# A two-layer streaming encoder on one core: the loop over MLP groups in pairs, squares on ScalarE with a tree of additions, xlo moved by 64 bytes, GpSimd's lower halves in four pieces, and later stores of x

## The chip, the cores and the metric

The kernel runs on one core of a Trainium2 chip. The metric is the device time of one execution in microseconds, and lower is better. The engines are TensorE (PE in the profile; PEld is its loading of weights), VectorE (DVE), ScalarE (ACT), GpSimd (POOL) and SyncE (SP), which here only issues transfers. They run side by side, each with its own instruction stream, and meet at semaphores.

## The reference, cut to what matters

```python
def rms_norm(x, g):
    return x * rsqrt(mean(x * x, axis=-1) + 1e-6) * g

# for each of DEPTH = 2 layers; x is 256 prompt rows and 64 sample rows of 2048
h = rms_norm(x, g_mix)
A | B | C | D = split(h @ w_in)              # four groups of attention heads, four kinds of attention
x = x + concat(oa, ob, oc, od) @ w_out
x = x + square(relu(rms_norm(x, g_mlp) @ w_up)) @ w_down        # 2048 -> 8192 -> 2048
x = x + (ple @ w_ple) * sigmoid(rms_norm(x, g_ple) @ w_ple_gate)
```

All is float32. The three norms need, for each of the 320 rows, the sum of 2048 squares; the division by the root comes after the product with the weights, so the matmuls can start on x times the gain.

## The kernel before, in words

**Layout.** x is feature-major: 16 blocks (KB) of 128 features on the partitions, each with 320 columns (TOK: 256 prompt and 64 sample rows), so 5120 floats or 20480 bytes in each partition. A float32 product is made of three matmuls in fp32r on a high and a low half of both operands (`product`, L695 to L697): low weight half by high x half, high by low, high by high. The upper half of the weights is made by ScalarE (`whi`, a Copy that rounds, L1130), the lower by GpSimd (`wlo = ring - whi`, L659). xhi and xlo are made by VectorE (`split_blocks`, L1351 and L1354), hhi and hlo in the MLP's up projection (L1752 and a product, L1313), pleh and plel for the embeddings.

**Where the halves lie.** xlo starts at 4 x KB x TOK = 20480 bytes behind xhi. plel starts 2560 bytes behind pleh. Adding up the allocations between them, hlo starts 145344 bytes behind hhi. xhi, xlo and the buffers of the attention share memory; the end of xlo meets the start of probT.

**Weights.** SyncE loads them as units of 512 KB into `ring`, which has four slots (RING). The layer's list of units (STREAM) starts with the 12 units of group A's columns of w_in (N_UP = 12), then come B, D, C, the latent weights and w_out, 108 units in all (TAIL0); the tail is 300 units: the end of w_out, the MLP, w_ple and w_ple_gate. In the head (up to TAIL0) a slot is loaded again when PE has used its unit, and the lower half is made in place, in pieces of 256 columns (`lower_in_place`, L646). In the tail a slot is loaded again as soon as both halves are made. ScalarE converts up to three units ahead of PE.

**The order on SyncE** is written out by hand in `beside`: ahead of the load of unit 4 stand 25 small loads of vectors and caches, and ahead of the loads of units SAVE_AT to SAVE_AT + 3 (5 to 8) stands one store of four blocks of x to DRAM each (L547). x is needed again when w_out is added (loaded back at BACK_AT), and the first copy of B's columns (`copy_chunk` for chunk 2) overwrites it, so that waits for the stores.

**A layer** runs so. (1) ScalarE makes xw, the rounded x times the gain, VectorE makes xv, its low half (L1324, L1326). Then VectorE takes the first squares: one product over all 5120 columns into the arena, one reduction over the 16 blocks (L1339) and a short copy. PE needs this sum after unit 7. Group A is copied out by VectorE (L1375, L1377), ScalarE squares it for its norm (L1144), and PE waits for that norm before it prepares the heads. ScalarE converts the units up to N_UP + LEAD - 1 = 14 before it takes those squares. (2) Attention in eight jobs, with matmuls for the other groups between. (3) The end of w_out, split and squares for the MLP. (4) The MLP in four groups of 2048 hidden features (FG = 4): a loop on each engine, and in each group four chunks of up (8 units each, `gemm_chunk`) and four of down. A unit is 24 matmuls. PE's loop body for one group is 1536 matmuls, each with its load of weights. VectorE's loop over the groups has a base for its step counter (`here`, UP_STEPS). (5) The embeddings (four units), then the gate in four chunks: meanwhile VectorE splits x again, and after that takes the squares (`squares_pass`: a product over 5120 columns, L1313, and a reduction, L1345). PE needs this sum after the gate's first chunk (`rms_feature`, L739).

Of the kernel before, what the change touches and what calls it, by code (L numbers as in the profile page):

```python
# [16 lines left out]
TOK = SEQ + DSEQ  # L17
# [6 lines left out]
KB = DM // 128  # L24
UK = 2
XW = 256 + 128
RING = 4
FG = FF // DM
# [34 lines left out]
def build(nc, I, O):  # L63
    f32 = mybir.dt.float32
    ALU, ACT, AX = mybir.AluOpType, mybir.ActivationFunctionType, mybir.AxisListType
    X = AX.X
    ctx = ExitStack()
    with ctx:
# [13 lines left out]
        def sem(name):  # L82
            return ctx.enter_context(nc.semaphore(name))
# [26 lines left out]
        xlo = sb("xlo", [128, KB, TOK], f32r, at + 4 * KB * TOK)  # L110
        assert at + 8 * KB * TOK <= top[0]
# [85 lines left out]
        sq_ready = sem("sq_ready")  # L197
        ssq_ready = sem("ssq_ready")
# [137 lines left out]
        SAVE_AT = RING + 1  # L336
# [291 lines left out]
        def _(pool):  # L628
# [9 lines left out]
            with pool.Fori(0, DEPTH) as l:  # L638
# [18 lines left out]
                def lower_half(u4, s):  # L657
                    hold(hi_ready, l * HL + N_WU + RING * u4 + s + 1)
                    nc.gpsimd.tensor_tensor(wlo[:, s, :], ring[:, s, :], whi[:, s, :].bitcast(f32), ALU.subtract)\  # L659
                        .then_inc(lo_ready, 1)  # L660
# [13 lines left out]
        def _(pe):  # L674
# [306 lines left out]
            with pe.Fori(0, DEPTH) as l:  # L981
# [43 lines left out]
                with pe.Fori(0, FG) as g:  # L1025
# [78 lines left out]
        def _(act):  # L1104
# [149 lines left out]
            with act.Fori(0, DEPTH) as l:  # L1254
                act.wait_ge(mix_loaded, 16 * (l + 1))
                gain_pass(l)
                halves(l, range(4, 11))
# [30 lines left out]
                for i in range(9):  # L1288
                    upper_halves(l, Q_PLE + i)
                    if i and i % 2 == 1 and i > 2:  # L1290
                        c = (i - 3) // 2
                        if c == 0:
                            rms_root(l, 1 + FG, ps[:, 7, 0:TOK], rroot[:, :])
                        sigmoids(l, c)
# [4 lines left out]
        def _(dve):  # L1299
# [35 lines left out]

            def first_squares(l):

                done(mul(plout, x[:, :, :], x[:, :, :]))
                done(V.tensor_reduce(acc[:, 0:TOK], plout.rearrange("p b t -> p t b"), X, ALU.add))  # L1339
                V.tensor_copy(acc[:, TOK:], acc[:, 256:TOK]).then_inc(acc_ready, 1)  # L1340

            def squares_pass(l, chunks):
                dve.wait_ge(half_free, l * CHUNKS + 2 + chunks)
                done(mul(hid[:, :, :], x[:, :, :], x[:, :, :]))
                V.tensor_reduce(acc[:, 0:TOK], hid[:, :, :].rearrange("p b t -> p t b"), X, ALU.add).then_inc(acc_ready, 1)  # L1345
# [322 lines left out]
            with dve.Fori(0, DEPTH) as l:  # L1668
# [64 lines left out]
                UP_STEPS = 2 * KB - 4  # L1733
                with dve.Fori(0, FG) as g:
                    here[0] = l * STEPS + g * UP_STEPS
                    at0 = count[0]
# [17 lines left out]
                    assert count[0] - at0 == UP_STEPS  # L1754
                    for c in range(4):
                        add_chunk(l, MLP0 + 32 + 64 * g + 8 * c, 8 + 8 * g + c, c % 2, 4 * c)
                here[0] = l * STEPS
                count[0] += (FG - 1) * UP_STEPS

# [12 lines left out]
                squares_pass(l, 4 + 8 * FG)  # L1772
# [85 lines left out]
```

## Time and profile before

| | |
|---|---|
| Median of 3 runs | 3578.41 us (3575.25 to 3582.28) |
| The profiled execution | 3571.53 us, its span 3569.7 us |
| PE busy | 3371.3 us, 94% of the span |
| DVE, ACT, POOL busy | 1417.0, 1124.7, 1898.2 us |
| Mean granted clock of PE | 0.966 of full speed |
| Chain that ended last, by engine | PE 85%, DVE 7%, issue 4% |

The profile is of one execution. The granted clock has two levels here, 1.2 and 2.4 GHz. The busy time of a matmul overlaps the next one's, so the pace of PE is read from the starts. "Issue" as a releaser means that the engine waited for nothing that the profile shows. Layer 0 is in the span from about 30 to 1789 us, layer 1 from there to 3556.

### The profile page before, as it was taken

The page shows a single profiled execution, that of the slowest core. Times are in us where ns is not written, and L with a number is a line of the kernel's source. Part 1 is how long each engine was busy: PE and PEld are TensorE (multiplying, and loading weights), DVE is VectorE, ACT ScalarE, POOL GpSimd, SP SyncE. Part 2 cuts the span into 40 slices and gives each one's busy share as a digit, 9 for nine tenths or more (in the row PEclk, how much of TensorE's full clock was granted, in tenths as well). Part 3 has the DMA queues.
Part 4 walks back from the last instruction along what each step waited for, and adds up shares of the span by engine and source line. Part 5 has one row for each costly group of instructions (what it writes and reads, how often), then busy time and mean ns, then how long its engine had stood idle before and what let it go on. Part 6 is the DMA issues. An engine that isn't in the chain of part 4 may idle for free.

```text
span 3569.7 us, 58680 instructions
## 1 busy us (share of the span) xinstructions
PE 3371.3 (94%) x20676; PEld 3041.9 (85%) x20676; DVE 1417.0 (40%) x2287; ACT 1124.7 (32%) x1614; POOL 1898.2 (53%) x1189
## 2 busy tenths in 40 slices
PE   7999989999999999999979998989999999999988
PEld 5776756699999999998967776667999999999988
DVE  5334554473052240525362345445621503305163
ACT  2333332333333323332333332313323333333322
POOL 4554200267667676677565551002776676666664
PEclk9999998999999999999989999989999999999999
DMA  5343322244454444544343333223544444445433
GB/s 167 104 118 102 113 66 80 81 137 152 142 148 153 137 153 142 148 154 142 116 136 112 115 95 101 75 71 93 148 154 141 149 154 140 150 144 151 151 122 119
DMA packets 295728, 453.18 MB, mean 127 GB/s; under 512 B 36336, under 2 KB 111344, under 8 KB 294832
## 3 DMA queue, kind: packets, MB, share of 16 engines
q1 hardware_dynamic: 295328, 448.66, 41.2%
q8 instruction: 190, 3.11, 0.3%
q0 software_dynamic: 144, 0.87, 0.1%
q14 instruction: 66, 0.54, 0.0%
HBM read 435.54 MB, written 14.06 MB: 126 GB/s over the span
## 4 chain that ended last, share of the span: by engine, by line
PE 85%; DVE 7%; issue 4%; ACT 1%; DMA 1%; SPq 1%; POOL 0%; DVEq 0%; ACTq 0%; POOLq 0%
PE ps L697 19%; PE ps L696 19%; PE ps L695 19%; PE ps L793 5%; PE ps L781 5%; PE ps L756 4%; PE ps L759 4%; PE ps L758 3%; PE ps L885 1%; DMA ring<-in_w_in 1%; DVE xhi L1351 1%; PE ps L831 1%; PE ps L920 1%; PE ps L889 1%; DVE xlo L1354 1%
## 5 line engine op out<-in xcount | busy, mean ns | idle before, releaser
L659 POOL TENSOR_TENSOR wlo<-ring,whi 128x1024 fp32r<-128x1024 f32 x600 | 1478.1, 2465 | 1256.4 <-ACT whi L1130 1256.4
L1130 ACT ACTIVATE whi<-ring 128x1024 fp32r<-128x1024 f32 x600 | 635.0, 1060 | 1420.9 <-PE ps L697 1420.9
L695 PE MATMUL ps<-xhi,wlo 128*128 128x320 f32 x2560 | 801.6, 313 | 23.4 <-issue 16.4
L696 PE MATMUL ps<-xlo,whi 128*128 128x320 f32 x2560 | 796.5, 311 | 0.0
L697 PE MATMUL ps<-xhi,whi 128*128 128x320 f32 x2560 | 796.4, 311 | 0.0
L697 PE MATMUL ps<-hhi,whi 128*128 128x320 f32 x2176 | 675.5, 310 | 0.0
L695 PE MATMUL ps<-hhi,wlo 128*128 128x320 f32 x2176 | 663.1, 305 | 6.0 <-DVE plel L1727 6.0
L696 PE MATMUL ps<-hlo,whi 128*128 128x320 f32 x2048 | 629.8, 308 | 0.0
L646 POOL TENSOR_TENSOR rlo<-ring,whi 128x256 fp32r<-128x256 f32 (+2 forms) x576 | 416.3, 755 | 371.6 <-ACT whi L1114 371.1
L695 PEld LDWEIGHTS ps<-xhi,wlo 128*128 128x128 f32 x2560 | 485.9, 190 | 28.8 <-issue 27.0
L696 PEld LDWEIGHTS ps<-xlo,whi 128*128 128x128 f32 x2560 | 486.0, 190 | 1.0 <-issue 0.4
L697 PEld LDWEIGHTS ps<-xhi,whi 128*128 128x128 f32 x2560 | 485.4, 190 | 0.0
L756 PE MATMUL ps<-rlo,xw 128*128 128x512 f32 (+3 forms) x1056 | 370.2, 356 | 50.0 <-POOL rlo L646 20.8
L695 PEld LDWEIGHTS ps<-hhi,wlo 128*128 128x128 f32 x2176 | 411.6, 189 | 6.6 <-issue 6.5
L1316 DVE TENSOR_TENSOR x<-ps,x 128x320 f32<-128x320 f32 x224 | 107.1, 487 | 777.6 <-PE ps L697 751.5
L697 PEld LDWEIGHTS ps<-hhi,whi 128*128 128x128 f32 x2176 | 411.3, 189 | 0.0
L696 PEld LDWEIGHTS ps<-hlo,whi 128*128 128x128 f32 x2048 | 383.0, 187 | 0.0
L759 PE MATMUL ps<-whi,xw 128*128 128x512 f32 (+3 forms) x1056 | 361.9, 348 | 0.0
L1313 DVE TENSOR_TENSOR hhi<-t 128x320 fp32r<-128x320 f32 x128 | 290.4, 2269 | 4.4
L756 PEld LDWEIGHTS ps<-rlo,xw 128*128 128x128 f32 x1056 | 204.1, 193 | 83.8 <-issue 60.0
L758 PE MATMUL ps<-whi,xv 128*128 128x512 f32 (+3 forms) x704 | 247.6, 352 | 0.0
L781 PE MATMUL ps<-hid,ring 128*128 128x320 f32 x768 | 231.9, 459 | 6.9 <-ACT vtok L1173 3.0
(243 smaller groups left out, 3170.8 us busy)
## 6 DMA issues: line engine op xcount, KB each, us to landing
ring<-in_w_up SPq DMA_DIRECT2D x256, 512.0 KB, 3.7
ring<-in_w_down SPq DMA_DIRECT2D x256, 512.0 KB, 3.6
ring<-in_w_in SPq DMA_DIRECT2D x120, 512.0 KB, 3.6
ring<-in_w_out SPq DMA_DIRECT2D x64, 512.0 KB, 3.9
ring<-in_w_ple_gate SPq DMA_DIRECT2D x64, 512.0 KB, 3.6
xsave<-x SPq DMA_DIRECT2D x8, 640.0 KB, 7.4
x<-xsave SPq DMA_DIRECT2D x8, 640.0 KB, 5.1
ring<-in_w_in SPq DMA_DIRECT2D x16, 288.0 KB, 2.8
```

The costliest lines, as they stand in the source:

```text
L646: last = nc.gpsimd.tensor_tensor(rlo[:, s, c:c + w], ring[:, s, c:c + w], whi[:, s, c:c + w].bitcast(f32), ALU.subtract)
L659: nc.gpsimd.tensor_tensor(wlo[:, s, :], ring[:, s, :], whi[:, s, :].bitcast(f32), ALU.subtract)\
L695: mm(out, lo[:, k, cols], xh, start=start, stop=False)
L696: mm(out, hi[:, k, cols], xl, start=False, stop=False)
L697: return mm(out, hi[:, k, cols], xh, start=False, stop=stop)
L756: mm(out, head, lo[:, k, :], start=(kk == 0), stop=False)
L758: mm(out, xv[:, kk, t * 128:(t + 1) * 128], hi[:, k, :], start=False, stop=False)
L759: last = mm(out, head, hi[:, k, :], start=False, stop=(kk == KB - 1))
L781: last = mm(ps[:, out_bank(b), 0:TOK], w[:, k - k0, c:c + 128], hid[:, k, :], start=(k == k0), stop=(k == k1 - 1))
L793: return nc.tensor.transpose(out, in_, ident[0:in_.shape[0], 0:in_.shape[0]])
L1130: A(whi[:, s, :], ring[:, s, :], ACT.Copy).then_inc(hi_ready, 1)
L1313: return V.tensor_tensor(out, a, b, ALU.mult)
```

## The change

Seven edits:

- xlo starts 64 bytes later.
- The stores of x stand ahead of the loads of units 12 to 15 in place of 5 to 8.
- In the tail, GpSimd makes the lower half of a unit in four pieces of 256 columns in place of one of 1024; the last one signals.
- PE's loop over the MLP's four groups runs twice over a body of two groups.
- The first squares are taken by ScalarE in four pieces of four blocks, each after the conversion of one of the units 4 to 7. VectorE then adds them up in a tree of four additions: 8, 4, 2 and 1 block wide.
- The squares ahead of the gate are taken by ScalarE in four pieces too, after the conversion of the four embedding units and when x is complete; the tree on VectorE. The squares ahead of the MLP keep their product on VectorE and get the tree for the reduction.
- VectorE's loop over the MLP's groups is written out.

```diff
-        xlo = sb("xlo", [128, KB, TOK], f32r, at + 4 * KB * TOK)
+        xlo = sb("xlo", [128, KB, TOK], f32r, at + 4 * KB * TOK + 64)
...
-        SAVE_AT = RING + 1
+        SAVE_AT = N_UP
...
-                    nc.gpsimd.tensor_tensor(wlo[:, s, :], ring[:, s, :], whi[:, s, :].bitcast(f32), ALU.subtract)\
-                        .then_inc(lo_ready, 1)
+                    for c in range(0, 1024, LO_COLS):
+                        last = nc.gpsimd.tensor_tensor(wlo[:, s, c:c + LO_COLS], ring[:, s, c:c + LO_COLS],
+                                                       whi[:, s, c:c + LO_COLS].bitcast(f32), ALU.subtract)
+                    last.then_inc(lo_ready, 1)
...
-                with pe.Fori(0, FG) as g:
+                with pe.Fori(0, FG // 2) as pair:
+                  for group in range(2):
+                    g = 2 * pair + group
...
-                halves(l, range(4, 11))
+                for q in range(4):
+                    halves(l, (4 + q,))
+                    A(plout[:, 4 * q:4 * q + 4, :], x[:, 4 * q:4 * q + 4, :], ACT.Square).then_inc(first_squared, 1)
+                halves(l, range(8, 11))
...
-                for i in range(9):
+                upper_halves(l, Q_PLE)
+                act.wait_ge(half_free, l * CHUNKS + 2 + 4 + 8 * FG)
+                for b in range(0, KB, 4):
+                    A(hid[:, b:b + 4, :], x[:, b:b + 4, :], ACT.Square).then_inc(gate_squares, 1)
+                for i in range(1, 9):
                     upper_halves(l, Q_PLE + i)
...
+            def add_blocks(sq16):
+
+                for n in (8, 4, 2):
+                    done(add(sq16[:, 0:n, :], sq16[:, 0:n, :], sq16[:, n:2 * n, :]))
+                return add(acc[:, 0:TOK], sq16[:, 0, :], sq16[:, 1, :])
+
             def first_squares(l):
 
-                done(mul(plout, x[:, :, :], x[:, :, :]))
-                done(V.tensor_reduce(acc[:, 0:TOK], plout.rearrange("p b t -> p t b"), X, ALU.add))
+                dve.wait_ge(first_squared, (l + 1) * 4)
+                done(add_blocks(plout))
                 V.tensor_copy(acc[:, TOK:], acc[:, 256:TOK]).then_inc(acc_ready, 1)
 
             def squares_pass(l, chunks):
                 dve.wait_ge(half_free, l * CHUNKS + 2 + chunks)
                 done(mul(hid[:, :, :], x[:, :, :], x[:, :, :]))
-                V.tensor_reduce(acc[:, 0:TOK], hid[:, :, :].rearrange("p b t -> p t b"), X, ALU.add).then_inc(acc_ready, 1)
+                add_blocks(hid).then_inc(acc_ready, 1)
...
-                UP_STEPS = 2 * KB - 4
-                with dve.Fori(0, FG) as g:
-                    here[0] = l * STEPS + g * UP_STEPS
-                    at0 = count[0]
+                for g in range(FG):
...
-                squares_pass(l, 4 + 8 * FG)
+                dve.wait_ge(gate_squares, (l + 1) * 4)
+                add_blocks(hid).then_inc(acc_ready, 1)
```

## Rows read from the trace of the kernel before

**Rows 1.** Waits of PE: waiting line, releaser, us in total, times, longest.

```profile
PE ps L739 <- DVE acc L1345: 21.0, 2, 10.5
PE ps L756 <- POOL rlo L646: 20.8, 8, 5.7
PE ps L695 <- issue: 16.4, 5, 3.5
```

**Rows 2.** Timeline of PE, three stretches: start us, us, engine, line, operation, tiles, [idle before].

```profile
789.81 0.31 PE L695 MATMUL ps<-xhi,wlo 128*128 128x320 f32 x1
...
809.90 0.31 PE L697 MATMUL ps<-xhi,whi 128*128 128x320 f32 x1
...
919.78 0.30 PE L695 MATMUL ps<-hhi,wlo 128*128 128x320 f32 x1
...
940.00 0.31 PE L697 MATMUL ps<-hhi,whi 128*128 128x320 f32 x1
...
1643.76 0.31 PE L695 MATMUL ps<-pleh,wlo 128*128 128x320 f32 x1
...
1648.16 0.31 PE L695 MATMUL ps<-pleh,wlo 128*128 128x320 f32 x1
```

**Rows 3.** Timeline of PE where group 1 of the MLP begins.

```profile
953.86 0.31 PE L697 MATMUL ps<-hhi,whi 128*128 128x320 f32 x1
957.69 0.38 PE L695 MATMUL ps<-xhi,wlo 128*128 128x320 f32 x1 [3.52 <-issue]
...
962.95 0.31 PE L696 MATMUL ps<-xlo,whi 128*128 128x320 f32 x1
```

**Rows 4.** Timeline of VectorE: a split beside idle GpSimd, and the gate's.

```profile
722.18 0.68 DVE L1351 TENSOR_SCALAR xhi<-x,gains 128x320 fp32r<-128x320 f32 x2
722.90 1.01 DVE L1354 SCALAR_TENSOR_TENSOR xlo<-x,gains,xhi 128x320 fp32r<-128x320 f32 x2
...
1651.41 0.68 DVE L1351 TENSOR_SCALAR xhi<-x,gains 128x320 fp32r<-128x320 f32 x2
...
1684.71 5.48 DVE L1313 TENSOR_TENSOR hid<-x 128x5120 f32<-128x5120 f32 x1
1690.23 8.83 DVE L1345 TENSOR_REDUCE acc<-hid 128x320 f32<-128x5120 f32 x1
```

**Rows 5.** Groups by form: count, busy us, mean ns, idle before.

```profile
L695 PE MATMUL ps<-xhi,wlo 128*128 128x320 f32 x2560 | 801.6, 313 | 23.4 <-issue 16.4 <-POOL wlo L659 3.8 <-DVE xlo L1354 2.8
...
L659 POOL TENSOR_TENSOR wlo<-ring,whi 128x1024 fp32r<-128x1024 f32 x600 | 1478.1, 2465 | 1256.4 <-ACT whi L1130 1256.4
L646 POOL TENSOR_TENSOR rlo<-ring,whi 128x256 fp32r<-128x256 f32 x544 | 409.1, 783 | 371.6 <-ACT whi L1114 371.1
```

**Rows 6.** Timeline of all engines at the start of layer 1.

```profile
1805.15 1.42 SPq L458 DMA_DIRECT2D ring<-in_w_in  x1
...
1810.67 1.06 ACT L1114 ACTIVATE whi<-ring 128x1024 fp32r<-128x1024 f32 x1 [7.10 <-DMA ring<-in_w_in]
1811.06 5.48 DVE L1313 TENSOR_TENSOR arena<-x 128x5120 f32<-128x5120 f32 x1
1811.91 5.21 POOL L646 TENSOR_TENSOR rlo<-ring,whi 128x256 fp32r<-128x256 f32 x1 [5.60 <-ACT whi L1114]
...
1819.61 0.77 PE L756 MATMUL ps<-rlo,xw 128*128 128x512 f32 x1 [5.74 <-POOL rlo L646]
...
1825.18 0.39 PE L759 MATMUL ps<-whi,xw 128*128 128x512 f32 x1
```

**Rows 7.** Page, issues of transfers: count, KB each, median us to landing.

```profile
ring<-in_w_in SPq DMA_DIRECT2D x120, 512.0 KB, 3.6
```

**Rows 8.** Timeline of ScalarE and VectorE where group A ends in layer 1.

```profile
1852.84 1.06 ACT L1114 ACTIVATE whi<-ring 128x1024 fp32r<-128x1024 f32 x1 [2.71 <-DMA ring<-in_w_in]
1853.51 0.49 DVE L1377 SCALAR_TENSOR_TENSOR proj_ac<-ps,rtok,proj_ac 64x256 f32<-64x256 f32 x1
1854.03 1.81 ACT L1144 ACTIVATE prob<-proj_ac 128x1920 f32<-128x1920 f32 x1
```

## What the change will do to the time

> **What bounds the kernel now.** TensorE (PE) is busy in 94% of the span and carries 85% of the chain that ended last, so I read the profile in this order: who PE waits for, how fast PE goes while it waits for nobody, and what happens around each long wait. The waits of PE [rows 1] show three things that this change touches. Two waits of 10.5 us for the sum of squares ahead of the gate (L739 for acc, once a layer). Five waits at L695, 16.4 us, that end in "issue", so in nothing that the profile shows: they stand before the first matmul of a new MLP group. There are six such boundaries, 3 in each layer; the sixth looks the same and is put down to a piece of GpSimd that ended in that moment. And eight waits for GpSimd's lower halves in the head, the longest 5.7 us. The rest of the MLP is PE without a gap.
>
> **Part 1, xlo 64 bytes on.** Between its first and last shown start, the up projection (xhi, xlo) makes 137 steps in 20.09 us, or 146.6 ns a matmul; the down projection (hhi, hlo) makes 140 steps in 20.22 us, or 144.4 ns; the embeddings (pleh, plel) make 30 in 4.40 us, 146.7 ns [rows 2]. All three have the same shape, the same weight tiles and the full clock. What differs is the distance from the high to the low half: 20480 and 2560 bytes for the slow pairs, both multiples of 128, and 145344 bytes, 64 beyond one, for the fast pair. The change puts xlo 64 bytes beyond a multiple of 128 too. Matmuls on xhi and xlo: 3 lines x 2560 [rows 5] = 7680, times 2.2 ns = 17 us, all on the path, less about 1 us where the gate's first chunk waits for its halves: 16. It is a reading of three tile pairs, so the other end is 0.
> A rule speaks against it. The Trainium skill, "SBUF — State Buffer", section "SBUF: two separate sides", says that on the engines' side only the port pair shared by VectorE and GpSimd causes contention and that PE never waits on anyone; by it 64 bytes are worth nothing, and the rows' 2.2 ns have another cause.
>
> **Part 2, the paired loop.** The last matmul of group 0 starts at 953.86 and the next at 957.69; a step is 0.14, so 3.69 us are lost. Then the clock is low for a while: 25 steps take 5.26 us, not 25 x 0.1466 = 3.67, another 1.6 us [rows 3]. The waits average 3.3 us [rows 1]; with 0.17 for the modelled end and 1.7 for the clock each boundary costs 5.2 us. Inside a group, from chunk to chunk, there is no such wait, with the same waits on semaphores; what the boundary has alone is the jump back of PE's loop over some 3000 instructions. Unrolled in pairs, one jump back is left of three in each layer: 4 x 5.2 = 21 us less. Ends: 0 if the group's start, not the jump, costs it, and 22. VectorE's loop is written out in full; its own jumps lie in its idle time, so nothing.
>
> **Part 3, squares ahead of the gate.** VectorE splits x from 1651.41 to 1684.7, then multiplies (5.48) and reduces (8.83) to 1699.06 [rows 4]; PE has waited since 1688.7, 10.5 us before. After: ScalarE squares in four pieces of 1280 columns. Its 1920 columns take 1.81 us [rows 8], so about 1.25 each, 5 us in all, put in at about 1645, as soon as x is complete; they delay the next upper half by some 3 us, which PE wants 7 us later. Off the path. VectorE adds 2560, 1280, 640 and 320 columns: at 5.48 us for 5120, that is 2.74 + 1.4 + 0.7 + 0.5 = 5.35 us, and each addition may wait for a piece of GpSimd, up to 0.7: I take 7.3.
> The splits before them quicken by part 4: a pair of blocks takes 0.68 + 1.01 us when GpSimd is idle (722.18, 722.90), and 8 pairs with 8 copies take 33.3 us here [rows 4]. With pieces of 0.7 instead of 2.4 us I take 0.3 a pair, 2.5 us. Then acc is ready at 1699.1 - 2.5 - 14.3 + 7.3 = 1689.6. PE comes at 1688.7 less 1.1 (faster steps, shorter waits for halves), so a wait of about 2 us is left. Gain per layer 9.5, both 19. Ends: 6.3 a layer if the splits stay and every addition waits in full; 12 if PE waits no more and the low clock behind the wait (1 us) goes too. The squares ahead of the MLP keep their product on VectorE and get the additions; L739 waits only at the two gates [rows 1], so nothing there.
>
> **Part 4, GpSimd in four pieces.** 600 instructions of 2465 ns become 2400 of which the head's in-place ones, same size, take 783 ns on average with contention [rows 5]: 3.1 us a unit, plus about 0.12 between. PE takes 24 x 0.1444 = 3.47 us a unit and GpSimd runs three units ahead, so this is hidden; it costs only if that cover goes (rival 3). What it gives is shorter waits for VectorE: in part 3, and at the MLP's start, where PE waits 3 us a layer for VectorE's splits and the halves of the embeddings. There a stall of 2.4 is replaced by more but short ones; 0.5 a layer, 1 in all. Ends: -3 and +9.
>
> **Part 5, first squares and the stores of x.** In layer 1, VectorE's product of 5120 columns starts at 1811.06 and one piece of GpSimd of 256 columns that meets it takes 5.21 instead of 0.7 us; PE starts unit 4 at 1819.61 after 5.74 us, at low clock: 13 steps to 1825.18 take 5.57 us where 0.227 each would be 3.0 [rows 6]. Both causes go. ScalarE takes the squares, between upper halves, where it waits for loads anyway. And the stores, queued on SyncE directly behind the loads of units 4 to 7, no longer share the DMA: unit 4's load took 5.5 us from its issue to ScalarE [rows 6], the median is 3.6 [rows 7]. Only 0.5 of that is safe, since the issue itself took 1.42. With a conversion of 1.06 and four pieces of 0.7 PE starts at 1814.3: 5.3 us, and 2.6 of low clock. Against it, the additions of 2.74 and 1.4 us now meet GpSimd in unit 7 and may hold it some 2.5 us. Layer 1: 5.4 (0 to 8). Layer 0 is bound by SyncE's issues: 0.5. In sum 6. The sum of squares comes later after the last unit than before, but PE asks for it only after unit 7, at about 1829 in layer 1.
> The stores now stand ahead of the loads of units 12 to 15. Queued behind them on SyncE are those loads and A's stores. ScalarE converts unit 14 before it squares for A's norm, and PE waits for that norm: the conversion begins at 1852.84, the squares at 1854.03, just as VectorE's last part of A arrives at 1854.0 [rows 8]: no slack. A load with a store behind it lands 0.5 to 3 us later; 1 a layer, 2 us back. Ends 0 and 6. VectorE waits for the stores ahead of its copy of B, some 50 us later: nothing.
>
> **Sum.** 16 + 21 + 19 + 1 + 6 - 2 = 61, less 1 for overlap: 60 us. The profiled execution took 3571.5 us (span 3569.7), the median is 3578.4, 6.9 above; I keep that distance: 3571.5 - 60 = 3511.5, as a median 3518.4.
>
> **Rivals.** (1) The 64 bytes do nothing: the three tile pairs differ in something else. For it: just three pairs. Against: both slow pairs agree to 0.1 ns in different parts of memory. 3518.4 + 16 = 3534. The page named above gives the same. (2) The boundary's wait stays because it belongs to starting a group (reads of the next group's registers, waits). For: the profile names no cause. Against: chunks start without it. 3518.4 + 21 = 3539. (3) Slower: GpSimd becomes the bound of the 600 tail units. It decides from (3.47 - 0.12)/4 = 0.84 us a piece, and it eats the gain of 60 at 0.1 us a unit more, about 0.86 a piece. VectorE takes turns with it through its multiplications in the up projection; if pieces then take 0.91 throughout, a unit takes 3.75 us, and 600 x 0.28 = 168 us are added: 3686. Against: 783 ns on average where VectorE was busy all the time. (4) More: the MLP's start and the gate lose their waits wholly, and unit 7 isn't held: 3 + 8 + 5 more, 3502.
>
> **How the numbers follow.** Forecast 0.70, rival 1 0.12, rival 2 0.07, rival 3 0.03, rival 4 0.06, the rest (new waits in the head or another bound) 0.02. The range runs from rival 4 with a little more, 3500, to rival 2, 3541. 0.2% (7 us) is about what a measurement of this kernel can tell from no change. Faster 0.95; same 0.02; slower 0.03.
>
> **What would show it.** Steps of xhi and xlo at 144.4 ns; waits of PE for "issue" at the MLP's boundaries, 2 instead of 6; the wait at L739 near 2 us; GpSimd's pieces under 0.84 us with gaps before them; unit 4 of layer 1 without a wait; ScalarE's unit 14 after VectorE's last part of A. The prediction is wrong if PE waits for wlo in the MLP, if A's norm starts over 3 us late, or if the steps stay at 146.6.

## The result and the profile after

The changed kernel takes 3529.82 us (median of 4 runs, 3522.98 to 3530.55); the kernel before took 3576.83 in the same comparison. The ratio is 0.9867 (in brackets, here and below, its 95% interval: [0.9854, 0.9879]), so 47 us less. The forecast was 3518.4 with a range from 3500 to 3541. The profiled executions went from a span of 3569.7 to one of 3527.6 us, 42.1 us less, where 60 were forecast. The sum can therefore be followed place by place, in one scale: how much earlier or later the same matmul starts. Each row of the table is what that stretch alone added.

| Stretch | forecast, us | measured, us |
|---|---|---|
| Layer 0, to the tail's first matmul that reads hlast (693.92 before, 699.87 after) | +0.5 | +5.9 |
| MLP's start, both layers: end of w_out, then chunk 0 of group 0 | -1.8 | -2.1 +5.4, -2.5 +5.4 = +6.2 |
| Chunks 1 to 3 of the eight up projections | -10.2 | +1.7 |
| Boundary and chunk 0, where the loop's jump went (4) | -22.7 | -5.7 -5.3 -5.5 -5.1 = -21.6 |
| Boundary and chunk 0, where the jump is still there (2) | -0.8 | -5.0 -1.4 = -6.4 |
| Gates, both layers | -21.4 | -11.3 -12.1 = -23.4 |
| Layer 1, to the same matmul of the tail | -4.4 | -6.2 +1.6 = -4.6 |
| Sum | -60.8 | -42.2 |

The forecast column is the prediction's sum, with part 1's 16 us given to the stretches by their matmuls: 0.4 us for a chunk 0, 1.27 for the three chunks behind it, 1.2 at a gate; the 1 us taken off for overlap is given to none.

**Who PE waits for now.** Waits of PE, columns as in [rows 1]:

```profile
PE ps L760 <- POOL rlo L648: 15.3, 7, 4.5
PE ps L699 <- POOL wlo L662: 7.2, 2, 3.7
PE ps L743 <- DVE acc L1329: 6.7, 2, 3.3
PE ps L699 <- DVE plel L1746: 4.7, 2, 2.3
PE ps L699 <- issue: 4.0, 2, 2.1
```

Against [rows 1], the gate's wait is 3.3 in place of 10.5, and "issue" has two waits of 2.0 us on average in place of five of 3.3. The second line stands at a new place: GpSimd's lower halves at the MLP's start, once a layer.

**The new wait.** Timelines of VectorE, GpSimd and PE at the MLP's start in layer 0:

```profile
740.54 6.03 DVE L1326 TENSOR_TENSOR hid<-x 128x5120 f32<-128x5120 f32 x1
746.61 6.45 DVE L1329 TENSOR_TENSOR hid<-hid 128x2560 f32<-128x2560 f32 x3
753.10 0.90 DVE L1329 TENSOR_TENSOR acc<-hid 128x320 f32<-128x320 f32 x1
...
735.05 27.14 POOL L662 TENSOR_TENSOR wlo<-ring,whi 128x256 fp32r<-128x256 f32 x23 [0.66 <-ACT whi L1136]
...
754.97 0.38 PE L699 MATMUL ps<-xhi,wlo 128*128 128x320 f32 x1 [3.51 <-POOL wlo L662]
```

VectorE is in the product and the tree from 740.54 to 754.00. GpSimd is never idle in its 27 us and yet makes only 23 pieces, 5.75 units, where PE uses a unit in 3.5 us, 7.7 in that time. PE has eaten the lead of three units by then and waits 3.5 us.

**The gate.** VectorE and PE, layer 0:

```profile
1659.06 1.65 DVE L1370 TENSOR_SCALAR xhi<-x,gains 128x320 fp32r<-128x320 f32 x2
1660.74 1.86 DVE L1373 SCALAR_TENSOR_TENSOR xlo<-x,gains,xhi 128x320 fp32r<-128x320 f32 x2
...
1676.40 6.57 DVE L1329 TENSOR_TENSOR hid<-hid 128x2560 f32<-128x2560 f32 x3
1683.00 0.90 DVE L1329 TENSOR_TENSOR acc<-hid 128x320 f32<-128x320 f32 x1
...
1684.05 1.18 PE L743 MATMUL ps<-acc,ones 128*128 128x320 f32 x2 [3.33 <-DVE acc L1329]
```

The tree takes 7.5 us where the product and the reduction took 14.4 [rows 4]. A pair of blocks takes 3.47 us (1659.06 to the next one's start at 1662.53), as long as PE takes for the unit that needs it.

**A boundary without and with the jump.** Inside a pair the last matmul of the down projection and the first of the next up projection are 0.15 us apart. Where the jump is left (L699, layer 0) the timeline of PE shows:

```profile
1187.86 0.31 PE L701 MATMUL ps<-hhi,whi 128*128 128x320 f32 x1
1190.07 0.38 PE L699 MATMUL ps<-xhi,wlo 128*128 128x320 f32 x1 [1.90 <-issue]
```

2.2 us between starts, where it was 3.83 in [rows 3].

**Layer 1's start.** ScalarE, VectorE and PE:

```profile
1794.39 1.26 ACT L1265 ACTIVATE arena<-x 128x1280 f32<-128x1280 f32 x1
...
1804.45 6.30 DVE L1329 TENSOR_TENSOR arena<-arena 128x2560 f32<-128x2560 f32 x3 [9.72 <-ACT arena L1265]
...
1810.46 0.47 PE L760 MATMUL ps<-rlo,xw 128*128 128x512 f32 x1 [1.21 <-POOL rlo L648]
...
1832.47 1.79 ACT L1150 ACTIVATE prob<-proj_ac 128x1920 f32<-128x1920 f32 x1
```

The wait of 5.74 us ahead of unit 4 [rows 6] is gone; one of 1.21 remains where the tree meets GpSimd.

**The pace of the up projection.** Four starts in group 1 of the MLP, first in chunk 0, then in chunk 1:

```profile
965.03 0.30 PE L699 MATMUL ps<-xhi,wlo 128*128 128x320 f32 x1
...
984.96 0.30 PE L699 MATMUL ps<-xhi,wlo 128*128 128x320 f32 x1
...
1000.09 0.31 PE L699 MATMUL ps<-xhi,wlo 128*128 128x320 f32 x1
...
1021.76 0.31 PE L699 MATMUL ps<-xhi,wlo 128*128 128x320 f32 x1
```

The first two are 138 steps apart, 144.4 ns each, as forecast. The last two are 147 steps apart, 147.4 ns each: slower than before the change (146.7, [rows 2]). The pace changes at one point in the group: the single matmul of acc on ones (L743) between chunk 0 and chunk 1. Seven of the eight groups do so; the chunks 0 behind a down projection and both gates' later chunks are at 144.4.

So the questions for the chip were: is each part worth what the sum gave it, where does the wait for wlo come from, and what decides between 144.4 and 147.4 ns.

### The profile page after: what moved, and what is told of

The parts are those of the page before. It is cut to its first block, busy times and chain, and to the rows that moved or that the text cites. A ratio compares the mean times of both kernels' runs of the same rounds, so it can differ in the third digit from the quotient of the medians.

```text
span 3527.6 us, 60466 instructions
## 1 busy us (share of the span) xinstructions
PE 3359.4 (95%) x20676; PEld 3030.3 (86%) x20676; DVE 1280.4 (36%) x2301; ACT 1143.7 (32%) x1630; POOL 2261.2 (64%) x2989
## 4 chain that ended last, share of the span: by engine, by line
PE 85%; DVE 6%; issue 4%; DMA 2%; ACT 2%; POOL 1%; SPq 1%; DVEq 0%; ACTq 0%; POOLq 0%
PE ps L700 19%; PE ps L701 19%; PE ps L699 19%; PE ps L797 5%; PE ps L785 5%; PE ps L760 4%; PE ps L763 4%; PE ps L762 3%; PE ps L889 1%; DMA ring<-in_w_in 1%; DVE xhi L1370 1%; PE ps L835 1%; PE ps L893 1%; PE ps L924 1%; PE ps L892 1%
## 5 line engine op out<-in xcount | busy, mean ns | idle before, releaser
L662 POOL TENSOR_TENSOR wlo<-ring,whi 128x256 fp32r<-128x256 f32 x2400 | 1836.5, 801 | 855.5 <-ACT whi L1136 855.0
L699 PE MATMUL ps<-xhi,wlo 128*128 128x320 f32 x2560 | 792.8, 310 | 11.2 <-POOL wlo L662 7.2
L699 PE MATMUL ps<-hhi,wlo 128*128 128x320 f32 x2176 | 661.6, 304 | 4.7 <-DVE plel L1746 4.7
L699 PEld LDWEIGHTS ps<-xhi,wlo 128*128 128x128 f32 x2560 | 486.6, 190 | 14.3 <-issue 12.5
L699 PEld LDWEIGHTS ps<-hhi,wlo 128*128 128x128 f32 x2176 | 410.4, 189 | 5.3 <-issue 5.1
L1120 ACT ACTIVATE whi<-ring 128x1024 fp32r<-128x1024 f32 (+2 forms) x152 | 147.5, 974 | 263.7 <-DMA ring<-in_w_in 223.5
```

The source lines that it names most:

```text
L662: last = nc.gpsimd.tensor_tensor(wlo[:, s, c:c + LO_COLS], ring[:, s, c:c + LO_COLS], whi[:, s, c:c + LO_COLS].bitcast(f32), ALU.subtract)
L699: mm(out, lo[:, k, cols], xh, start=start, stop=False)
L1120: A(whi[:, s, 0:nk * ncol], ring[:, s, 0:nk * ncol], ACT.Copy).then_inc(hi_ready, 1)
```

## The experiments

Unless another unit is given, times are medians in us, and a ratio is to the kernel before in the same comparison. The kernel before had medians of 3572.9, 3574.7, 3575.1 and 3571.0 in the four comparisons.

### One part at a time, on the kernel before

**xlo 64 bytes on, alone (b_xlo64).**

```diff
-        xlo = sb("xlo", [128, KB, TOK], f32r, at + 4 * KB * TOK)
+        xlo = sb("xlo", [128, KB, TOK], f32r, at + 4 * KB * TOK + 64)
```

> The kernel before with xlo 64 bytes on and nothing else. Theory of the prediction: every matmul of an up projection and of the gate steps in 144.4 instead of 146.7 ns, 16 us less. What the trace of the whole change suggests instead: the 64 bytes give 144.4 ns only in stretches, and the rest goes at 147.4; if that comes from the distance alone, it shows here as well, in the up projection's chunks 1 to 3, and the gain is 4 to 6 us. If another part of the change (pieces, pairs, tree) brings the 147.4, all of xhi and xlo steps in 144.4 here and the gain is 14 to 17 us.

Measured: 3571.99, ratio 0.9999 [0.9989, 1.0008], with single runs from 3561.0 to 3580.4. In the profiled execution, whose span is 3559.2, seven of eight groups are at 144.4 ns through chunks 1 to 3, one at 147.4, and the whole gate of layer 0 at 147.4. Two pairs of starts, group 1 and the gate of layer 0:

```profile
1009.70 0.30 PE L695 MATMUL ps<-xhi,wlo 128*128 128x320 f32 x1
...
1031.80 0.30 PE L695 MATMUL ps<-xhi,wlo 128*128 128x320 f32 x1
...
1719.81 0.31 PE L695 MATMUL ps<-xhi,wlo 128*128 128x320 f32 x1
...
1741.93 0.31 PE L695 MATMUL ps<-xhi,wlo 128*128 128x320 f32 x1
```

153 steps of 144.4 ns, then 150 of 147.5. Both paces thus come with the 64 bytes alone; none of the other parts is needed. This execution, the fastest of twelve, gained 10 us; the median gained nothing. The paces of the other eleven are not known.

**The paired loop, alone (b_pairs).**

```diff
-                with pe.Fori(0, FG) as g:
+                with pe.Fori(0, FG // 2) as pair:
+                  for group in range(2):
+                    g = 2 * pair + group
```

> The kernel before with the body of PE's loop written out for two groups and nothing else (VectorE keeps its loop). The jump back costs the wait: two of the six waits of 3.3 us at the MLP's boundaries are left, with the low clock behind them, 18 to 22 us less. The start of a group costs it: six waits, no change. A third reading, that VectorE's jump has a part in it: some boundaries keep a wait, 5 to 15 us less.

Measured: 3552.47, ratio 0.9938 [0.9925, 0.9951]: 20 us less. Two waits for "issue" are left, 7.0 us in all, and the four boundaries gained 5.3, 4.9, 5.0 and 4.8 us each with chunk 0. The jump it is, at 5.0 us where 5.2 were forecast; VectorE's loop, kept here, has no part in it.

**GpSimd in four pieces, alone (b_pieces).**

```diff
-                    nc.gpsimd.tensor_tensor(wlo[:, s, :], ring[:, s, :], whi[:, s, :].bitcast(f32), ALU.subtract)\
-                        .then_inc(lo_ready, 1)
+                    for c in range(0, 1024, LO_COLS):
+                        last = nc.gpsimd.tensor_tensor(wlo[:, s, c:c + LO_COLS], ...
+                    last.then_inc(lo_ready, 1)
```

> The kernel before with GpSimd's lower halves of the tail in four pieces and nothing else. The prediction put it at 1 us less at the MLP's start and 5 us less at the two gates (the splits take turns with pieces of 0.7 in place of 2.4 us): 6 us less. Rival, from the new waits for wlo in the changed kernel: a product or an addition of 2 to 6 us on VectorE now holds up GpSimd for each piece in turn; then PE waits for wlo ahead of the MLP here as well (the product is there, the tree is not: one piece held for 5.5 us), and the gain is 0 to 3 us. Steps of xhi and xlo: 146.7 ns unless the pieces act on them.

Measured: 3555.92, ratio 0.9942 [0.9929, 0.9955]: 17 us less, three times the 6 of the forecast. Place by place: the gates 4.2 and 4.2 us; PE waits 8.8 there. The six boundaries of the loop: 7.4 us together, five of them shorter and one 0.9 longer. The waits for "issue" are 2.3 us on average (2.0 to 3.0) in place of 3.3, and the low clock behind them is shorter in part. Here is the one of [rows 3] again:

```profile
953.24 0.31 PE L699 MATMUL ps<-hhi,whi 128*128 128x320 f32 x1
...
955.95 0.55 PE L697 MATMUL ps<-xhi,wlo 128*128 128x320 f32 x1 [2.40 <-issue]
```

No wait for wlo ahead of the MLP, where the reduction still stands: the rival in the expectation falls. Why the boundary's wait shrinks, no run tells; its steps stay at 146.7 ns.

**The gate's squares on ScalarE with the tree, alone (b_gate).**

```diff
-                for i in range(9):
+                upper_halves(l, Q_PLE)
+                act.wait_ge(half_free, l * CHUNKS + 2 + 4 + 8 * FG)
+                for b in range(0, KB, 4):
+                    A(hid[:, b:b + 4, :], x[:, b:b + 4, :], ACT.Square).then_inc(gate_squares, 1)
+                for i in range(1, 9):
...
-                squares_pass(l, 4 + 8 * FG)
+                dve.wait_ge(gate_squares, (l + 1) * 4)
+                add_blocks(hid).then_inc(acc_ready, 1)
```

> The kernel before with the gate's squares taken by ScalarE and added up in the tree, and nothing else (whole pieces of 1024 columns on GpSimd). The prediction's working without the help of the pieces: the wait ahead of L739's successor falls from 10.5 to between 2 and 6 us, since each of the four additions may have to wait for a GpSimd operation of 1.7 us: 5 to 8 us a layer, 10 to 16 in all. If the tree does as well without the pieces as with them (wait 3.3), 14 to 16; if each addition waits in full, 8 to 10.

Measured: 3569.19, ratio 0.9993 [0.9983, 1.0002], 6 us less at most, under every number of the expectation. The wait for acc did fall, to 6.0 us. But a new one of 3.2 stands in front of the gate. GpSimd, VectorE, PE, layer 0:

```profile
1651.53 7.38 POOL L660 TENSOR_TENSOR wlo<-ring,whi 128x1024 fp32r<-128x1024 f32 x3 [3.17 <-ACT whi L1131]
...
1652.15 4.45 DVE L1362 TENSOR_SCALAR xhi<-x,gains 128x320 fp32r<-128x320 f32 x2
...
1661.95 0.38 PE L696 MATMUL ps<-xhi,wlo 128*128 128x320 f32 x1 [3.21 <-DVE arena L1775]
```

ScalarE's 4.7 us of squares hold back the upper halves, GpSimd then has three whole units in a row, and they come just as VectorE begins to split: 4.45 us in place of 0.68 [rows 4]. The copy that frees the bank for the gate (L1775) is queued behind that on VectorE. I had put the squares off the path because PE wants the delayed upper half 7 us later; the one who paid was VectorE, by way of GpSimd. And a whole piece of GpSimd takes 2.3 us or more (2337 ns is the shortest of the 600 in the kernel before), not the 1.7 of my expectation.

The four medians add up to 42 us (0.9 + 20.4 + 17.0 + 3.7), with the first squares and the stores not among them; the whole change gains 47. The parts are not additive in their places, as the next run shows.

### One part taken back, on the changed kernel

**The reduction back ahead of the MLP (a_reduce).** In `squares_pass`, which only the MLP uses now:

```diff
-                add_blocks(hid).then_inc(acc_ready, 1)
+                V.tensor_reduce(acc[:, 0:TOK], hid[:, :, :].rearrange("p b t -> p t b"), X, ALU.add).then_inc(acc_ready, 1)
```

> The changed kernel, but the squares ahead of the MLP are added up by VectorE's one reduction again, not by the tree. Theory: the tree's additions, with two operands in SBUF, held up GpSimd's pieces, so that PE waited 3.5 and 3.7 us for wlo and then ran at the low clock; the reduction lets GpSimd run. Expected: no wait for wlo ahead of the MLP, 5.4 us less a layer, 8 to 11 us less than the changed kernel, about 3520. Rival: the product alone (6 us) is enough, or the pieces are: the wait for wlo stays at over 2 us, and the time at 3527 to 3530.

Measured: 3511.57, ratio 0.9823 [0.9809, 0.9837]: 18 us less than the changed kernel by the medians, 16 by the two ratios, 14 by the spans. The waits for wlo are gone, and chunk 0 of group 0 is 5.7 us shorter in both layers. Four groups more are at 144.4, another 6.6 us; one gate more is slow, and the head of layer 1, where nothing differs, took 3.8 us longer in this execution. The busy time of GpSimd in 13.4 us behind the start of VectorE's product, first in the changed kernel, then here (stretch: length, busy us (instructions), granted clock, share of DMA, GB/s):

```profile
740.60:754.00 13.40, 13.40 (x6) 1.00 0.22 71
```

```profile
739.60:753.00 13.40, 13.40 (x12) 1.00 0.35 110
```

Busy all the time in both, but six pieces beside the product and the tree, twelve beside the product and the reduction. Without the product, which both have and which lets two pieces through in either, beside the tree (changed kernel) and beside the reduction (here):

```profile
746.70:754.00 7.30, 7.30 (x5) 1.00 0.25 72
```

```profile
745.60:753.00 7.40, 7.40 (x11) 1.00 0.48 143
```

GpSimd's "busy" holds its waiting: a busy share says nothing about progress. The Trainium skill, "SBUF — State Buffer", section "SBUF: two separate sides", says that a VectorE operation with two inputs in SBUF takes the port pair that it shares with GpSimd for its whole length, and under "Who interferes with whom" that a reduction on this chip never contends with GpSimd. The trace agrees, 5 pieces against 11.

**Whole pieces again (a_whole).** The inverse of b_pieces' edit.

> The changed kernel, but GpSimd makes the tail's lower halves in one piece of 1024 again. The runs so far say that the pieces were the cover of the gate's new order: with whole pieces ScalarE's squares bunch up three pieces of GpSimd, which hold the gate's first split (a new wait of PE of 3.2 us), and the additions wait 6 us in place of 3.3. Theory: both come back, and each boundary of the loop costs 1.2 us more: the two gates cost 16 us more, in all 14 to 22 us slower than the changed kernel, less what the MLP's start gives back if its stall comes from the pieces (up to 11 us). Rival: the pieces matter little, within 5 us.

Measured: 3543.91, ratio 0.9911 [0.9895, 0.9928]: 14 us slower than the changed kernel by the medians, 16 by the ratios. The two gates cost 8.3 us each (a new wait of 3.2 ahead of each, and 6.7 in place of 3.3 ahead of the sum's matmul), and the two boundaries with a jump 6.6 together. At the MLP's start the embeddings' wait is longer again (3.0 in place of 2.3, 2.0 and 2.3 us with the clock), and chunk 0 of group 0 gives back 5.0 and 4.9. Waits of PE, and GpSimd beside the product and the tree (columns as above):

```profile
PE ps L741 <- DVE acc L1327: 13.4, 2, 6.7
PE ps L697 <- DVE arena L1775: 6.4, 2, 3.2
```

```profile
742.50:762.00 19.50, 19.42 (x5) 1.00 0.37 107
```

Product and tree take 19.6 us here, 13.5 with pieces, and still PE hardly starves: it waits 0.42 and 0.35 us for wlo in chunk 0, where the changed kernel waits 3.5 and 3.7. Five operations of GpSimd are five whole units. The two engines take turns, one operation each. A turn is worth a unit when GpSimd's operation is a unit, and a quarter of it when it is a piece. So neither the tree nor the pieces make the stall of 3.5 us alone; b_pieces has the pieces without it, a_whole the tree without it, and the change has both.

**The stores of x early again (a_save).**

```diff
-        SAVE_AT = N_UP
+        SAVE_AT = RING + 1
```

> The changed kernel with the stores of x ahead of the loads of units 5 to 8 again. The prediction had their move at 2 us lost where group A ends, and an uncertain part of the 5.4 us gained at layer 1's start. Theory: the norm of A comes 0.5 to 2 us earlier in each layer, while unit 4 of layer 1 comes 1 to 2.5 us later: within 3 us of the changed kernel. Rival: the move is what made layer 1's start shorter: 4 to 6 us slower.

Measured: 3524.70, ratio 0.9854 [0.9834, 0.9875], not to be told from the changed kernel; the rival falls. The local effect is plain. From PE's matmuls on the first sum (L992) to ScalarE's squares for A's norm (L1150), layer 1:

```profile
1817.74 0.72 PE L992 MATMUL ps<-ones,acc 128*128 128x1 f32 x6
...
1835.00 1.81 ACT L1150 ACTIVATE prob<-proj_ac 128x1920 f32<-128x1920 f32 x1
```

17.26 us; 17.26 in layer 0 too (73.84 to 91.10), and 17.25 and 17.26 in the kernel before. The changed kernel has 1814.19 to 1832.47 and 72.57 to 90.92: 18.28 and 18.35. The later stores cost 1.0 and 1.1 us there, the forecast's 1 a layer. They give something at the layer's start: from layer 1's first matmul to its first on the sum it is 36.3 us here, and 33.3 to 35.6 in the eight kernels with the later stores. That is some 1 to 3 us, from one execution.

### What decides the pace

The paces below are mean steps between the starts of neighbouring matmuls, over stretches of 20 us in every chunk. "Slow" counts the up projections whose chunks 1 to 3 are at the slow pace.

| xlo's distance beyond a multiple of 512 | fast | slow | slow, of those behind a matmul of acc |
|---|---|---|---|
| 0 (before, and the three kernels on it without part 1) | - | 146.7 | 32 of 32 |
| 64 (b_xlo64, the changed kernel, a_reduce, a_whole, a_save, c_early) | 144.4 | 147.4 | 1, 7, 3, 5, 4, 8 of 8 |
| 64, the matmul in groups 0 and 2 only (c_half) | 144.4 | 147.4 | 1 of 4 |
| 448 (a_xlo448) | 144.4 | 146.7 | 4 of 8 |
| 32 (a_xlo32) | 144.4 | 145.5 | 5 of 8 |

**xlo 448 bytes on (a_xlo448).** `+ 448` in place of `+ 64`.

> The changed kernel with xlo 448 bytes on in place of 64, which makes its distance from xhi equal modulo 512 to that of hlo from hhi (also modulo 128: 64). Theory A: the distance modulo 512 is what makes the down projection go steadily at 144.4 ns; then the up projection's chunks 1 to 3 do too, 1.7 us less in each of the 7 slow groups: 12 us less than the changed kernel. Theory B: only modulo 128 counts, and fast or slow is settled anew at each start of a stretch: some groups at 144.4, some at 147.4, the time within 8 us of the changed kernel and spread from run to run.

Measured: 3526.53, ratio 0.9863 [0.9847, 0.9879]. Theory A falls: half of the groups are slow, though now at 146.7. The time agrees with B, but its "modulo 128" falls too: 64 and 448 are equal modulo 128 and have different slow paces. And one thing neither said: now the down projection, which with every other distance goes at 144.4 in all its groups, is at 146.7 in four of eight, and these are the four behind a slow up projection. Its pair has the same distance modulo 512 (448). Here a pace, once taken, is carried from one pair into the next: the one up projection that follows such a down projection without a jump is at 146.7 from its chunk 0. With 64 or 32 bytes it isn't. There the down projection behind a slow up projection goes at 144.4 to 144.5, and the chunk 0 behind that, where no jump stands between, at 144.4. So with distances that differ modulo 512 the change of operands ends the slow pace as well. Only xlo was moved, by 32, 64 and 448 bytes: that the distance counts and not xlo's own place rests on the two other pairs, and that it counts modulo 512, rather than 256, on no run.

**xlo 32 bytes on (a_xlo32), with the reduction.**

> The changed kernel with the reduction ahead of the MLP and xlo 32 bytes on in place of 64. The down projection's pair and the changed xhi and xlo both have 64 beyond a multiple of 128, and xhi and xlo alone fall into 147.4 now and then; with 448 bytes they had 144.4 or 146.7. Theory: any distance off a multiple of 128 lets the fast pace come, and the slow one depends on the rest of the distance: the slow pace at 32 is then another than 147.4. Rival: 32 bytes are too few, and xhi and xlo go at 146.7 everywhere, 8 to 10 us slower than with the reduction alone.

Measured: 3510.32, ratio 0.9817 [0.9803, 0.9830]. The theory holds: the slow pace is 145.5 ns, one ns above the fast one. The time equals that of a_reduce within the intervals.

**The sum over the partitions only in groups 0 and 2 (c_half), with the reduction.**

```diff
-                                   before_last=(lambda: hold(rms_ready, l * N_RMS + g + 2)) if c == 1 else None)
-                        if c == 0:
+                                   before_last=(lambda: hold(rms_ready, l * N_RMS + pair + 2)) if (c, group) == (1, 0) else None)
+                        if (c, group) == (0, 0):
...
-                    dve.wait_ge(rms_ready, l * N_RMS + g + 2)
-                    V.reciprocal(rfeat[:, :], rroot[:, :]).then_inc(inv_ready, 1)
-                    dve.wait_ge(inv_ready, l * (FG + 1) + g + 1)
+                    if g % 2 == 0:
+                        dve.wait_ge(rms_ready, l * N_RMS + g // 2 + 2)
+                        V.reciprocal(rfeat[:, :], rroot[:, :]).then_inc(inv_ready, 1)
+                        dve.wait_ge(inv_ready, l * (FG // 2 + 1) + g // 2 + 1)
```

> The changed kernel with the reduction ahead of the MLP (as in the run before) and, new, the sum of squares over the partitions (one matmul of acc on ones, L743, and its root) made only in groups 0 and 2, since acc is the same in all four. Theory: the steps of xhi and xlo are settled anew at each such matmul, which stands between chunk 0 and chunk 1; after the down projection they begin at 144.4. So groups 1 and 3 of both layers go at 144.4 through all four chunks (8 of 8 cases fast), and groups 0 and 2 stay mixed: 2 to 6 us less than with the reduction alone (3511.6). Rival: fast and slow come by another cause (what ScalarE, GpSimd or VectorE do from chunk 1 on): groups 1 and 3 are at 147.4 in about half of the cases as well, and the time gains only the four matmuls, 1 us.

Measured: 3502.87, ratio 0.9797 [0.9784, 0.9811], 9 us less than a_reduce. Groups 1 and 3 of both layers are four cases, not the eight that I wrote, and all four stay at 144.4 through their four chunks. In the six kernels with 64 bytes and that matmul in every group, 28 of 48 groups are slow behind it; by these shares four of four at 144.4 have a chance of 3%, and c_best below has four more. The starts in group 1, at the place where the changed kernel has 147.4:

```profile
999.96 0.30 PE L699 MATMUL ps<-xhi,wlo 128*128 128x320 f32 x1
...
1021.62 0.30 PE L699 MATMUL ps<-xhi,wlo 128*128 128x320 f32 x1
```

150 steps of 144.4 ns. A break in the stream of matmuls settles the pace anew: this matmul, and also the jump of the loop (chunk 0 behind it is at 147.4 in one or both layers of b_xlo64, a_reduce, a_whole, a_save, c_early and this run). ScalarE's root and VectorE's reciprocal went with the matmul, so that these two as the cause are not ruled out. What about the break chooses is open. By the profiled executions, which are 12.6 us apart, groups 1 and 3 are 0.72 us shorter each than those at 144.4 in a_reduce (2.9 in all), two groups fewer are slow (3.3), and the head of layer 1 ran 3.9 us faster, where nothing differs.

### A better version

**The gate's splits earlier (c_early), with the reduction.** x's blocks 4c to 4c + 3 are final after chunk c of the last down projection, and xhi and xlo are free by then.

```diff
+                        if g == FG - 1:
+                            dve.wait_ge(half_free, l * CHUNKS + 2 + 4 + 8 * g + 4 + c + 1)
+                            split_blocks(2, 4 * c, 4 * c + 4)
...
-                add_blocks(hid).then_inc(acc_ready, 1)
+                V.tensor_reduce(acc[:, 0:TOK], hid[:, :, :].rearrange("p b t -> p t b"), X, ALU.add).then_inc(acc_ready, 1)
```

> The changed kernel with the reduction ahead of the MLP and, new, the gate's splits taken in the last group's down projection, each four blocks as soon as x has them, and the gate's sum by the reduction right behind the last copy of the embeddings. Theory: the gate's wait (3.3 us) is VectorE's time for the splits, since they start late; they then end before the gate starts, PE waits for nothing there and keeps its clock: 3.3 us and up to 1 of low clock, twice, 7 to 9 us less than with the reduction alone (3511.6): 3503 to 3505. Rival: the splits meet GpSimd in the down projection and PE waits there for hlo or wlo instead: no gain, or 5 us slower.

Measured: 3501.28, ratio 0.9792 [0.9778, 0.9805], 10 us less than a_reduce, with single runs from 3494.1 to 3517.0 (in the profiled one, the slowest, all eight groups have the slow pace). The sum is there long before PE asks for it, at about 1677. VectorE, layer 0, and the waits of PE:

```profile
1649.81 9.51 DVE L1782 TENSOR_REDUCE acc<-hid 128x320 f32<-128x5120 f32 x1
```

```profile
PE ps L699 <- DVE plel L1746: 4.8, 2, 2.5
PE ps L699 <- issue: 3.9, 2, 2.2
PE ps L699 <- DVE arena L1779: 1.8, 2, 0.9
```

The line with acc is gone, and 0.9 us a layer came in its place, for copies behind the last split. The rival falls: the down projection has no new wait. The reduction at the gate came in the same run, so what it gave apart from the earlier splits isn't known.

**All of it, with 32 bytes (c_best).** The edits of a_reduce, c_half, c_early and a_xlo32 together.

> The changed kernel with what the runs so far show to pay: the reduction ahead of the MLP, the sum of squares only in groups 0 and 2, the gate's splits in the last group's down projection with the reduction behind the embeddings, and xlo 32 bytes on, whose slow pace is 145.5 in place of 147.4 ns. Theory: the parts act in different places and add up. From the run with the sums in two groups (3502.9): the gate's two waits of 3.3 us and what stands behind them, 7 to 9 us less, and up to 2 us for the pace: 3492 to 3496. Groups 1 and 3 of both layers (four cases) at 144.4 in all four chunks, the others at 144.4 or 145.5. Rival: the early splits bring VectorE and GpSimd together in the down projection and cost there what they save at the gate: 3500 to 3503.

Measured: 3493.90 (3493.52 to 3494.01), ratio 0.978 [0.9767, 0.9794]. It is 77 us faster than the kernel before, where the change gained 47, and its runs lie within 0.5 us of each other. Groups 1 and 3 are at 144.4 in all four cases, two of the four others at 145.5. What PE still waits for in the tail:

```profile
PE ps L699 <- DVE plel L1746: 4.7, 2, 2.3
PE ps L699 <- issue: 3.9, 2, 2.0
PE ps L699 <- DVE arena L1780: 1.8, 2, 0.9
```

## Why the prediction was right, and where it was not

The median lies in the range and the sign is right, but the gain was forecast at 60 and is 47 by the medians, 42 by the two profiles. Parts 2, 3 and 5 came about as the prediction has them. That the total came within 13 us is in part luck: two steps failed, for 20 us together, and 6 us at the loop's jumps, which no step had, paid for part of it. Step by step, with what each missed (a plus is time that I had not expected):

- **Part 1, xlo: 16 forecast, about 4 measured, +12.** The reading of [rows 2] was right as far as it went: the pace does depend on the distance, and 144.4 is to be had. The step that failed is "16 for 7680 matmuls": a fast pair seen in one place was taken for a constant of the distance. The three pairs could not show that a distance has two paces. At 64 the slow one is worse than the old constant one (147.4 against 146.7), which may be why the median of this edit alone is no gain; only one of its executions was profiled. The rule that the prediction cites from the Trainium skill, "SBUF — State Buffer", that PE never waits on anyone, gave zero. The pace of 144.4 in most of b_xlo64's up projections shows that the distance acts; whether a port has a part in it, no run shows. Rival 1's time, 3534, came closer than the forecast, but by another way than it said.
- **Part 2, the loop: 21 forecast.** The four boundaries gave 21.6 with chunk 0's pace and 20 without, b_pairs alone 20. Right in mechanism and size (+1); rival 2 falls. The two jumps that are left became cheaper by 5.6, net of the pace. b_pieces and a_whole put that on part 4, and the prediction had nothing of it: -6. Why is open.
- **Part 3, the gate: 19 forecast, 20 measured, the rest of the gates' 23.4 being pace and clock: -2.** The wait is 3.3, not 2, and the tree's 7.5 us were taken as 7.3. But the text let it stand by itself with the pieces giving 2.5 us, and b_gate shows that without the pieces it is worth at most 6 us in all. The number was right for the whole change, not for the part.
- **"The squares ahead of the MLP ... so nothing there": +8 at the MLP's start.** This is the other step that failed. It asked whether PE waits for acc there (it does not) and not what the tree does to GpSimd, though part 5 two paragraphs on has the additions hold GpSimd, and [rows 6] the price. The reduction was 9.6 us in which GpSimd went on; the tree with the product makes 13.4 us in which it gets six turns of a quarter unit. The prediction's own sign for this, PE waiting for wlo in the MLP, came true. Rival 3 had the right engine at the wrong place: GpSimd is the bound for some 14 us a layer, not for the tail. Its average, "783 ns where VectorE was busy all the time", hid this: 801 ns a piece over 2400 pieces, and 2.2 us in that stretch (13.4 over 6).
- **Part 4, at the MLP's start: 0.5 a layer forecast.** The stretch up to the up projection gained 2.1 and 2.5 (the embeddings' wait from 3.0 to 2.3 us, and the clock behind it), and the stall took 5.4 back in each layer. Alone, the pieces were worth 17 us, not 6: what they gave at the loop's boundaries was in no step.
- **Part 5: layer 1's head, 4.4 forecast, 4.6 measured**; the stores, 1 a layer forecast, 1.0 and 1.1 measured. Up to the first sum's matmul that head takes 38.3 to 39.8 us in the five kernels with the old code and 33.3 to 35.6 in the eight with the new one, 4.8 less on average where 5.4 was forecast. The rest of it runs from 622.9 to 629.7 us among these eight, so that two profiles agree with the forecast to 0.2 us by luck.
- **Layer 0's head: 0.5 more forecast, 5.9 measured, +5.** A good part of it isn't the change. b_xlo64, b_pairs, b_pieces and b_gate have the same code there as the kernel before, and the same matmul of the tail starts at 697.4, 698.9, 695.6 and 695.5, and at 693.9 in the kernel before; the kernels with the change's head have it from 697.3 to 700.4. The profile of before is the lowest of the five, by 1.5 to 5 us. What is left, some 2 to 3 us, may be the change's; it was not tried apart. It also goes some way to explain why the medians gained 47 and the profiles 42.

In sum: +12 (pace of chunks 1 to 3), +8 (MLP's start), +5 (head of layer 0), +1 (boundaries without a jump), -6 (those with one), -2 (gates) make 18, the distance between 60 and 42.

## What to carry to other kernels

When an operation is replaced by a faster one on the same engine, ask what the old one left free: a slower reduction that lets GpSimd run beat a faster tree that takes its turns, and the finer GpSimd's pieces are, the less of its work fits into a turn; check it by counting instructions in the stretch, not by busy time. A pace read from a few tile pairs is a sample: look at every stretch of such matmuls, and at the spread of runs, before multiplying by thousands. And a cover that hides one part may be made by another (here the pieces for the gate), so price the parts together with what they rest on.

## What the runs showed of the hardware that I had not expected

- Two paces of the same stream of matmuls (128x128 on 320 columns, weights loaded for each): 144.4 ns a step, and a slow one that goes with the distance between the two moving operands: 145.5 ns at 32 bytes beyond a multiple of 512, 147.4 at 64, 146.7 at 448. At 0 only 146.7 was seen. On the same two operands the pace lasts until the stream is broken by another kind of matmul or by the loop's jump, and may come out either way then. Into the next pair of operands it was carried where both distances are equal modulo 512 (a_xlo448), and not elsewhere.
- A jump back of PE's loop over some 3000 instructions costs 3.3 us of waiting, 5.0 with the low clock behind it (b_pairs), and 2.0 to 3.0 us of waiting when GpSimd works in small pieces (b_pieces; 1.7 to 2.2 in the changed kernels, whose body is twice as long). The cause of that difference is open.
- GpSimd and VectorE take turns operation by operation when both read two operands from SBUF: 6 pieces of 0.7 us in 13.4 us beside the product and the tree, 12 beside the product and the reduction.
